# Modulation slots taken in the inverse and ahead of the output matrix, and a first expert that starts without its lead-in

## The chip, the cores and the metric

The kernel runs on one core of one Trainium2 chip. The metric is the device time of one execution in microseconds (us); the figure compared is the median over executions. Five engines share the work: TensorE (PE, with PEld for its weight loads), VectorE (DVE), ScalarE (ACT), GpSimd (POOL) and SyncE (SP), whose queue issues every transfer from memory.

## The reference, cut to what matters

One token sequence (256 tokens, width 1024, fp32) goes through a first block (modulated norm, a gMLP half and an RWKV-7 half, output matrix, router, 32 experts) and then through a two-layer second block (attention and feed-forward). The parts that the change touches:

```
mod = c @ ada_w + ada_b                       # first block's modulation, 1 x 6144
mod2 = silu(c_2) @ w_mod_2[i] + b_mod_2[i]    # second block's, layer i, 1 x 6144
...
state = state * w_t + sa * b_t + v_t * k_t    # RWKV-7, done in chunks of 64 tokens:
                                              # an inverse per chunk and head, then 4 chunks in turn
y = concat(y_a, y_b) @ w_out
x = x + gate1 * y
h = modulate(rmsnorm(x), shift2, scale2)
# router: best group of 4, best 2 experts of its 8, slots sorted by expert
y_e = (silu(xb @ w_gate[e]) * (xb @ w_up[e])) @ w_down[e]      # 32 experts, 6.3 MB of weights each
x = x + gate2 * sum(weights * y_e)
```

## The kernel before, in words

**Weights** stream through a ring of six 2 MB slots (`ring`), filled by SP in one fixed order (`load`, line 302) and used by TensorE in the same order (`take`). Load n waits until `slot_freed` has counted n-5. The first matmul of the next slot's use frees the slot before it (`opened`), so a slot taken earlier lets a later load start earlier. The order of loads is: four of `ada_w`, five of `w_in` and a small one, eight of `ada_w` (numbers 10 to 17), two of `w_mod0`, two of `w_out`, two more of `w_mod0`, then the experts' matrices (`load_matrix`, lines 353 and 366). Each expert has gate, up and down, 2 MB each. The experts use nine places, the six of the ring and three `wide` pairs in the arena, so that the first three experts are loaded before any is freed; the refill of a place waits for the use that follows it.

**Modulation.** A modulation vector is a product with one column, cut in slots: `mod_slice` (line 591) does eight narrow matmuls on one 2 MB slot into bank 0 (`part`), and `fill(n)` does the next n slots wherever it is called. After every fourth slot ScalarE copies the bank (`part_copy`, line 2219), TensorE turns the copy to columns (`flush`, line 604) and VectorE adds the bias (`mod_columns`, line 1506); the first slot of the next four waits for that (`mod_copied`). Slots 4 to 11 are the first block's, 12 to 15 the second block's.

**The inverse** (`inverse`, products at line 783) doubles a block-triangular inverse in six levels l = 0 to 5, for two halves T of 128 tokens. At each level TensorE makes two products that VectorE masks (line 1658, `p_ready`), and after these two or four more that VectorE adds up (lines 1664 and 1667). Engines alternate by semaphores.

**The recurrence** is a chain: `u_of(c)` (line 838), `p_first_half` (827), `v_terms` (811), `d_state` (847), `p_state` (819), `y_state` (863), `y_v` (857), `y_u` (871), each followed by a copy on VectorE (`pb_of`, `u_of`, `state_of`, `y_of`). Fills and flushes stand between them. After it come the group norm's sums (905, 919), the router's small products (911, 914), the output matrix (939 on the gMLP half, 948 on the RWKV half), and the router: logits (975), turned (980), two fills (591), ranks (986 to 990) once VectorE has the one-hots (1781), and one flush.

**The experts.** Tokens are gathered by products into eight chunks (`gather`, 997), ScalarE copies each into `xsT` (2328), and before the first expert `gathered` clears banks 4 to 7 by products with zeros (`add_y` with `first`, 1038). Then `expert(i, e)` reads two numbers from `mtab` (1089, 1090) and runs `window`: gate and up products (1050), the combination of the expert before (`add_y`, 1038), turned activations (1071) and the down product. VectorE copies the window's tokens to `xw` at the start of its `act_pass` (1838). `frees` are the semaphores that tell SP of a free place; that of the up matrix is sent by the first down product. Experts 0 to 4 are written out, the others run in loops of three.

Of the kernel before, what the change touches and what calls it, by code (L numbers as in the profile page):

```python
# [19 lines left out]
ACT = mybir.ActivationFunctionType  # L20
AX = mybir.AxisListType

P = 128
# [3 lines left out]
DC = D // P  # L27
# [5 lines left out]
NE, HID = 32, 512  # L33
# [76 lines left out]
def build_program(nc, a):  # L110
    with ExitStack() as ctx:
# [184 lines left out]
        def _(sp):  # L296
# [36 lines left out]
            for i in range(2):  # L333
                load_mod("w_mod0", i)
            for i in range(2):
                load(w_cols(a["w_out"], 512 * i), 4096)
            for i in range(2, 4):
                load_mod("w_mod0", i)
# [224 lines left out]
        def _(pe):  # L563
# [352 lines left out]
            last.then_inc(S("logits_done"), 1)  # L916
            pe.wait_ge(S("ysq_ready"), 2)
# [35 lines left out]
            ahead[0] = True  # L953
# [28 lines left out]
            fill(2)  # L982
# [3 lines left out]
            mm(bank[6][:, 0:NE], upper[:, :], oh[:, 0], start=True, stop=True).then_inc(S("slot_freed"), 1)  # L986
# [26 lines left out]
            for c in range(4, DC):  # L1013
                pe.wait_ge(S("xs_copied"), c - 3)
                gather(c, 0)
                gather(c, 1).then_inc(S("xs_done"), 1)


            moe_n0 = st_pe.n
            pe.wait_ge(S("mtab_ready"), 1)  # L1020

            def gathered():

                pe.wait_ge(S("routes_copied"), 2)
                pe.wait_ge(S("ym_ready"), 1)
                pe.wait_ge(S("pwin_made"), 1)
                add_y(1, first=True)
                add_y(0, first=True, parts=(1,))
                pe.wait_ge(S("xs_copied"), 8)
                for name in ("up_done", "down_done", "act_turned"):  # L1030
                    pe.nop().then_inc(S(name), 1)
                add_y(0, first=True, parts=(0,))

            def add_y(t, first=False, name=None, parts=(0, 1)):

# [1540 lines left out]
```

## Time and profile before

| | us |
|---|---|
| median of 3 runs | 1507.18 |
| lowest, highest | 1506.53, 1508.94 |
| the profiled execution | 1503.41 |
| span of its instructions | 1501.7 |
| TensorE busy in the span | 1431.7 (95%) |
| VectorE busy | 613.2 (41%) |
| ScalarE busy | 245.1 (16%) |
| GpSimd busy | 210.6 (14%) |

The stages by the clock of the trace: inverse from 143 to 176, recurrence to 206, output matrix 215 to 244, router to 261, gather to 276, experts 280 to 727, second block to the end. TensorE's share says little by itself: in the experts a transfer can set the pace while TensorE is still busy nine tenths of the time. Idle time of TensorE is short everywhere, so the question at each place is what would be late next.

### The profile page before, as it was taken

To read this page: it belongs to the slowest core of one execution; us is meant where nothing else is said; L and a number is where in the kernel's file an instruction comes from. 1 tells how busy PE (TensorE), PEld (TensorE's weight loads), DVE (VectorE), ACT (ScalarE), POOL (GpSimd) and SP (SyncE) were. 2 spreads that over 40 slices of the span, in tenths; PEclk is the share of its full clock that TensorE was granted. 3 is DMA by queue.
4 is the path that set the end of the run, shared out by engine and by line. 5 is a ranking of instruction groups with operands and counts; after the bars stand their busy time and mean duration, and the time that the engine had idled before them with its cause. 6 is when DMAs were issued, how large, how long until landed. Compare 5 with 4: busy or idle time off the path is not lost.

```text
span 1501.7 us, 23350 instructions
## 1 busy us (share of the span) xinstructions
PE 1431.7 (95%) x9316; PEld 940.4 (63%) x9317; DVE 613.2 (41%) x1087; ACT 245.1 (16%) x496; POOL 210.6 (14%) x149
## 2 busy tenths in 40 slices
PE   6999999999999999999899999999999999999997
PEld 3867854544444444444486749998448664899943
DVE  1356544111111111111463425556665463455666
ACT  1230013200000000000301622001031052200001
POOL 2000000000000000000000027770000002577100
PEclk9999999999999999999999999999999999999999
DMA  9664295899999999999999245436426942352610
GB/s 375 242 253 182 74 378 199 329 426 421 425 425 427 423 425 425 424 425 427 409 393 370 79 137 216 153 132 233 164 87 233 402 179 80 105 209 72 236 58 29
DMA packets 91794, 400.91 MB, mean 267 GB/s; under 512 B 7329, under 2 KB 12577, under 8 KB 63553
## 3 DMA queue, kind: packets, MB, share of 16 engines
q1 hardware_dynamic: 91712, 399.73, 67.3%
q8 instruction: 63, 1.03, 0.3%
q14 instruction: 19, 0.15, 0.0%
HBM read 398.66 MB, written 1.05 MB: 266 GB/s over the span
## 4 chain that ended last, share of the span: by engine, by line
PE 78%; DMA 12%; DVE 6%; issue 1%; ACT 1%; SPq 1%; DVEq 0%; ACTq 0%
PE psum L1382 17%; PE psum L1050 16%; PE psum L1434 7%; PE psum L1196 5%; DMA arena<-in_moe_up 4%; PE psum L662 4%; PE psum L1344 4%; PE psum L1038 4%; DMA ring<-in_moe_up 2%; DMA arena<-in_moe_gate 2%; DMA arena<-in_w_mod 2%; PE psum L1414 2%; PE psum L591 2%; PE psum L783 2%; PE psum L1229 2%; PE psum L1214 2%
## 5 line engine op out<-in xcount | busy, mean ns | idle before, releaser
L1050 PE MATMUL psum<-ring,arena 128*64 128x256 f32 (+1 forms) x1760 | 241.4, 427 | 12.5 <-DMA ring<-in_moe_up 6.2
L1050 PEld LDWEIGHTS psum<-ring,arena 128*64 128x64 f32 x1760 | 127.3, 138 | 133.2 <-issue 61.0
L1382 PE MATMUL psum<-arena,ring 128*128 128x128 f32 x1280 | 150.4, 276 | 2.1 <-ACT arena L2198 2.0
L1382 PEld LDWEIGHTS psum<-arena,ring 128*128 128x128 f32 x1280 | 146.5, 192 | 2.8 <-issue 2.8
L1842 DVE TENSOR_TENSOR arena<-psum,arena 128x256 f32<-128x256 f32 x32 | 13.6, 425 | 257.2 <-PE psum L1050 257.2
L1050 PE MATMUL psum<-arena 128*64 128x256 f32 (+1 forms) x800 | 109.1, 425 | 5.1 <-DMA arena<-in_moe_up 3.3
L1382 PE MATMUL psum<-arena 128*128 128x128 f32 x960 | 113.9, 276 | 0.0
L1196 PE MATMUL psum<-arena,ring 128*128 128x256 f32 x512 | 112.7, 382 | 0.8 <-DVE arena L1493 0.7
L557 POOL TENSOR_TENSOR arena<-ring 128x1024 f32<-128x1024 f32 x20 | 47.1, 2353 | 459.1 <-PE psum L1344 242.5
L1382 PEld LDWEIGHTS psum<-arena 128*128 128x128 f32 x960 | 110.4, 192 | 0.0
L1196 PEld LDWEIGHTS psum<-arena,ring 128*128 128x128 f32 x512 | 97.6, 192 | 15.9 <-issue 3.1
L1434 PE MATMUL psum<-arena 128*128 128x512 f32 x220 | 99.3, 594 | 2.1 <-DVE arena L2131 2.1
L1050 PEld LDWEIGHTS psum<-arena 128*64 128x64 f32 x800 | 56.9, 137 | 60.3 <-issue 25.9
L1038 PE MATMUL psum<-arena 64*128 64x512 f32 x272 | 76.9, 640 | 0.7 <-ACT arena L2352 0.7
L1434 PEld LDWEIGHTS psum<-arena 128*128 128x128 f32 x220 | 41.6, 191 | 55.0 <-issue 54.9
L1929 DVE SCALAR_TENSOR_TENSOR arena<-arena,small 128x2048 f32<-128x2048 f32 x27 | 63.5, 2352 | 17.9 <-DMA arena<-in_w_mod 17.2
L2352 ACT ACTIVATE arena<-psum 128x512 f32<-128x512 f32 x32 | 19.1, 597 | 307.6 <-PE psum L1050 307.6
L529 POOL MEMSET arena<- 128x640 f32 x1 | 0.6, 631 | 479.7 <-DVE x L1881 479.7
L662 PE MATMUL psum<-arena,ring 128*128 128x256 f32 x256 | 58.1, 388 | 0.0
L1344 PE MATMUL psum<-ring,arena 128*128 128x512 f32 x128 | 55.5, 594 | 0.6 <-DVE arena L1975 0.6
L662 PEld LDWEIGHTS psum<-arena,ring 128*128 128x128 f32 x256 | 49.8, 195 | 8.4 <-issue 1.6
L1838 DVE COPY arena<-arena 128x512 f32 x32 | 13.7, 427 | 89.7 <-issue 79.1
(423 smaller groups left out, 1728.7 us busy)
## 6 DMA issues: line engine op xcount, KB each, us to landing
ring<-in_moe_gate SPq DMA_DIRECT2D x22, 2048.0 KB, 24.1
ring<-in_moe_up SPq DMA_DIRECT2D x22, 2048.0 KB, 22.7
ring<-in_moe_down SPq DMA_DIRECT2D x22, 2048.0 KB, 24.4
arena<-in_w_mod SPq DMA_DIRECT2D x32, 1024.0 KB, 9.6
ring<-in_ada_w SPq DMA_DIRECT2D x12, 2048.0 KB, 10.7
ring<-in_w_qkv SPq DMA_DIRECT2D x12, 2048.0 KB, 15.0
arena<-in_moe_gate SPq DMA_DIRECT2D x20, 1024.0 KB, 22.2
arena<-in_moe_up SPq DMA_DIRECT2D x20, 1024.0 KB, 20.8
```

Source lines behind the costliest of these rows:

```text
L557: g(nc.gpsimd.tensor_tensor(s1, w21, w22, ALU.add))
L591: last = mm(part[32 * g:32 * g + 1, :], vec[:, c:c + 1], w[:, cc, 512 * g:512 * g + 512], start=(c == 0), stop=(c == DC - 1), tile_positio ...
L662: last = mm(b[:, mi * TOK:(mi + 1) * TOK], w[:, c, m * P:(m + 1) * P], hT[:, c, :], start=(c == 0), stop=(c == DC - 1))
L783: last = mm(out[ps, j * CH:(j + 1) * CH], left(ps, j), right(ps, j), start=True, stop=True, tile_position=(ps.start, ps.start))
L1038: last = mm(bank[4 + 2 * t + n][:, :], pwin[hs, t * P:(t + 1) * P], ym[hs, :], start=first, stop=(name is not None), skip_group_check=True)
L1050: ins = mm(bank[b][o, 0:n], lhsT, w[:, half * n:(half + 1) * n], start=first, stop=last, tile_position=(0, 64 * half))
L1196: last = mm(bank[1 + u % 6][:, mi * TOK:(mi + 1) * TOK], w[:, c, m * P:(m + 1) * P], hTd[:, c, :], start=(c == 0), stop=(c == DC - 1))
L1214: last = mm(bank[1 + u % 6][:, :], hTd[:, c, t * P:(t + 1) * P], w[:, c, :], start=(c == 0), stop=(c == DC - 1))
L1344: last = mm(bank[1 + 2 * t + n][:, :], oT[:, c, t * P:(t + 1) * P], w[n][:, c, :], start=(c == 0), stop=(c == DC - 1))
L1382: last = mm(bank[b + k][:, slot * P:slot * P + P], left[:, k, c], right[:, c, :], start=(c == 0), stop=(c == 3))
L1434: last = mm(bank[t][:, :], *terms[t], start=(p == 0), stop=(p == PAIRS - 1))
L1929: ins = V.scalar_tensor_tensor(out=macc2, in0=w, scalar=by, in1=macc2, op0=ALU.mult, op1=ALU.add)
```

## The change

In the order of the program:

- SP loads all four `w_mod0` slots (numbers 18 to 21) before the two of `w_out` (22 and 23).
- In the inverse, TensorE does a fill between the two masked products of a level and the products behind them, at levels 0, 2, 3, 4 and 5, and the second flush at level 1. VectorE's `mod_columns` goes to level 1.
- The recurrence keeps one fill (slot 12) and one flush of the seven fills and two flushes that stood between line 838's first products and line 911 (slot 13 still stands behind 905). Its products stand in another order, and VectorE's copies with them.
- Slots 14 and 15 are filled before line 919, and the third block of columns is flushed behind 939. In the router four idle products stand in place of the two fills; nothing reads them.
- The gather of chunks 4 to 7 uses the banks in another turn, and the two `mtab` numbers of expert 0 are read before its last chunk. `gathered` is gone: VectorE clears banks 4 to 7 by memsets. The first gate product waits for seven copied chunks, its last eighth for the eighth.
- `act_pass` copies the tokens of the following window after its own multiplication, not its own window's at the start.
- The up matrix's place is told free by the first `add_y` product behind the up products.

```diff
-            for i in range(2):
+            for i in range(4):
                 load_mod("w_mod0", i)
             for i in range(2):
                 load(w_cols(a["w_out"], 512 * i), 4096)
-            for i in range(2, 4):
-                load_mod("w_mod0", i)
...
+                    if l == 1:
+                        flush()
+                    else:
+                        fill(1)
                     for T in range(NT):
                         pe.wait_ge(S("p_ready"), 2 * l + T + 1)
...
             u_of(0)
-            fill(1)
+            flush()
             p_first_half(0)
-            flush()
+            pe.wait_ge(S("xt_ready"), 12)
+            y_v(1)
             u_of(1)
-            pe.wait_ge(S("pb_ready"), 2)
             v_terms(1)
-            fill(1)
             d_state()
-            fill(1)
+            y_u(0)
             p_state()
-            y_u(0)
+            y_state()
             u_of(2)
-            y_v(1)
             fill(1)
             p_first_half(1)
-            y_state()
-            fill(1)
             u_of(3)
             y_u(1)
-            flush()
-            fill(1)
...
             last.then_inc(S("logits_done"), 1)
+            fill(2)
             pe.wait_ge(S("ysq_ready"), 2)
...
+            flush()
             rows(diag[:, 0], 1, 3)
...
-            fill(2)
+            idle_products(3, 4)
...
             rows(diag[:, 1], 2, 3)
-            flush()
...
-                return mm(bank[1 + c % 4][:, :], xr[:, t, :].rearrange("q (p c) -> q c p", c=DC)[:, c, :], perm[:, t, :],
+                return mm(bank[1 + (c + 3 * (c // 4)) % 4][:, :], xr[:, t, :].rearrange("q (p c) -> q c p", c=DC)[:, c, :], perm[:, t, :],
...
             for c in range(4, DC):
-                pe.wait_ge(S("xs_copied"), c - 3)
+                pe.wait_ge(S("xs_copied"), 4)
+                if c == DC - 1:
+                    pe.wait_ge(S("mtab_ready"), 1)
+                    extra0 = pe.value_load(mtab[0:1, NE:NE + 1], min_val=0, max_val=3)
+                    before0 = pe.value_load(mtab[0:1, 2 * NE:2 * NE + 1], min_val=1, max_val=4 * NE)
                 gather(c, 0)
                 gather(c, 1).then_inc(S("xs_done"), 1)
...
+                    if frees and n == 0:
+                        last.then_inc(S(frees), 1)
...
+                        if k == 0 and c == DC - 1:
+                            pe.wait_ge(S("xs_copied"), DC + 1)
                         last = product(1 + k, xw[:, c, :], w(c), 256, c == 0, c == DC - 1)
...
-                add_y(0)
+                add_y(0, frees=frees and frees[2])
...
-                    if frees and k == 0:
-                        last.then_inc(S(frees[2]), 1)
...
-            gathered()
...
+            d(V.memset(bank[6][:, :], 0.0))
+            dve.wait_ge(S("routes_copied"), 2)
+            for b in (5, 7):
+                d(V.memset(bank[b][:, :], 0.0))
+            dve.wait_ge(S("xs_copied"), 5)
+            d(V.memset(bank[4][:, :], 0.0))
             dve.nop().then_inc(S("pwin_made"), 1)
-            dve.wait_ge(S("routes_copied"), 2)
-
-            def act_pass(start, row, done):
-
-                dve.wait_ge(S("up_done"), done)
-                V.tensor_copy(xw, xsT[:, :, bass.ds(start, WIN)]).then_inc(S("xw_ready"), 1)
+
+            dve.wait_ge(S("xs_copied"), DC - 1)
+            V.tensor_copy(xw[:, 0:DC - 1, :], xsT[:, 0:DC - 1, 0:WIN]).then_inc(S("xw_ready"), 1)
+            dve.wait_ge(S("xs_copied"), DC)
+            V.tensor_copy(xw[:, DC - 1, :], xsT[:, DC - 1, 0:WIN]).then_inc(S("xs_copied"), 1)
+
+            def act_pass(following, row, done):
+
...
                 V.tensor_tensor(actm, bank[2][:, 0:4 * WIN], sg, ALU.mult).then_inc(S("act_done"), 1)
+                V.tensor_copy(xw, xsT[:, :, bass.ds(following, WIN)]).then_inc(S("xw_ready"), 1)
...
+            part_copy()
             row_copies(gate1b, 1, 3)
...
-            part_copy()
             row_copies(gate2b, 2, 3)
```

Three places on TensorE show how the rows stand. The first is the inverse up to its end. Line 783 (781 after) is the inverse's product, 591 (589) a fill, 604 (602) a flush, 838 (840) the first product of the recurrence. Before:

```order
L857 MATMUL psum<-arena 64x128 x8
L783 MATMUL psum<-ident,arena 64x64 x64
L783 MATMUL psum<-arena 64x64 x448
L838 MATMUL psum<-arena 64x64 x8
L591 MATMUL psum<-ring,cols 1x512 x8
L827 MATMUL psum<-arena 64x64 x8
```

After:

```order
L859 MATMUL psum<-arena 64x128 x8
L781 MATMUL psum<-ident,arena 64x64 x32
L589 MATMUL psum<-ring,cols 1x512 x8
L781 MATMUL psum<-ident,arena 64x64 x32
L781 MATMUL psum<-arena 64x64 x32
L602 MATMUL psum<-ident,macc 128x4 x4
L781 MATMUL psum<-arena 64x64 x96
L589 MATMUL psum<-ring,cols 1x512 x8
...
L781 MATMUL psum<-arena 64x64 x32
L840 MATMUL psum<-arena 64x64 x8
L602 MATMUL psum<-ident,macc 128x4 x4
```

Five fills and a flush now stand inside the inverse, and a flush stands behind the first product of the recurrence.

The second place is the end of the recurrence, up to the output matrix (939, after 936). 838 and 871 (840 and 873) are `u_of` and `y_u`, 905 and 919 (901 and 916) the group norm's sums. Before:

```order
L838 MATMUL psum<-arena 64x64 x8
L871 MATMUL psum<-arena 64x128 x8
L604 MATMUL psum<-ident,macc 128x4 x4
L591 MATMUL psum<-ring,small 1x512 x8
L905 MATMUL psum<-arena,bones 128x512 x2
L591 MATMUL psum<-ring,small 1x512 x8
L911 MATMUL psum<-modc,arena 128x16 x8
L914 MATMUL psum<-rw,modc 128x36 x8
L919 MATMUL psum<-arena,bones 128x512 x2
```

After:

```order
L589 MATMUL psum<-ring,small 1x512 x8
L829 MATMUL psum<-arena 64x64 x8
L840 MATMUL psum<-arena 64x64 x8
L873 MATMUL psum<-arena 64x128 x8
L901 MATMUL psum<-arena,bones 128x512 x2
L589 MATMUL psum<-ring,small 1x512 x8
L907 MATMUL psum<-modc,arena 128x16 x8
L910 MATMUL psum<-rw,modc 128x36 x8
L589 MATMUL psum<-ring,small 1x512 x16
L916 MATMUL psum<-arena,bones 128x512 x2
```

Nothing stands any more between 829, 840, 873 and 901, which wait for one another's copies on VectorE; two fills stand ahead of 916.

The third place is the last of the gather (997, after 993) and the first gate product (1050, after 1040). Before:

```order
L997 MATMUL psum<-arena 128x512 x8
L1038 MATMUL psum<-arena 128x512 x4
L1089 TENSOR_LOAD level
L1089 ISA x2
L1090 TENSOR_LOAD level
```

After:

```order
L993 MATMUL psum<-arena 128x512 x6
L1013 TENSOR_LOAD level
L1013 ISA x2
L1014 TENSOR_LOAD level
L1014 ISA x2
L993 MATMUL psum<-arena 128x512 x2
L1094 COMPARE_AND_BRANCH
L1095 UNCONDITIONAL_BRANCH
L1047 REGISTER_ALU
L1040 MATMUL psum<-ring,arena 64x256 x32
```

The four zero products are gone and the two loads of a number stand ahead of the last two gather products.

## Rows read from the trace of the kernel before

**Rows 1.** Chain of waits: start, us, what (the last transfer of the experts).

```profile
679.52 37.14 DMA ring<-in_moe_up
716.71 3.67 PE psum L1050 x32
```

**Rows 2.** Windows: stretch, length, busy (x instructions) by engine, clock, DMA share, GB/s.

```profile
290.00:292.00 2.00, 2.00 (x12) 0.63 (x10) 1.03 (x2) 0.00 (x0) 0.00 (x0) 1.00 0.69 295
292.00:294.00 2.00, 2.00 (x10) 0.43 (x6) 0.36 (x1) 0.00 (x0) 0.00 (x0) 1.00 0.68 197
...
566.00:727.00 161.00, 148.51 (x992) 74.44 (x990) 26.13 (x57) 11.22 (x23) 0.00 (x0) 1.00 1.01 424
```

**Rows 3.** Timeline of TensorE, a late expert: start, us, line, operation, count [idle before <-releaser].

```profile
627.81 3.67 PE L1050 MATMUL psum<-ring,arena 128*64 128x256 f32 x32 [1.02 <-DMA ring<-in_moe_up]
```

**Rows 4.** Timeline of SP's queue: the first refills of the ring.

```profile
284.99 0.33 SPq L353 DMA_DIRECT2D ring<-in_moe_gate  x1
291.59 0.33 SPq L353 DMA_DIRECT2D ring<-in_moe_up  x1
294.82 0.38 SPq L353 DMA_DIRECT2D ring<-in_moe_down  x1
```

**Rows 5.** Timeline of TensorE: the inverse, a fill and a flush.

```profile
146.28 1.15 PE L783 MATMUL psum<-ident,arena 64*64 64x64 f32 x32 [0.30 <-DVE arena L1658]
...
155.46 5.82 PE L783 MATMUL psum<-arena 64*64 64x64 f32 x192 [0.43 <-DVE arena L1658]
161.64 5.81 PE L783 MATMUL psum<-arena 64*64 64x64 f32 x192 [0.36 <-DVE arena L1658]
167.82 7.81 PE L783 MATMUL psum<-arena 64*64 64x64 f32 x256 [0.37 <-DVE arena L1658]
...
176.69 1.90 PE L591 MATMUL psum<-ring,cols 128*1 128x512 f32 x16
178.52 1.14 PE L827 MATMUL psum<-arena 64*64 64x64 f32 x16
179.59 1.05 PE L604 MATMUL psum<-ident,macc 128*128 128x4 f32 x8
```

**Rows 6.** Timeline of TensorE: the end of the recurrence.

```profile
201.24 1.09 PE L871 MATMUL psum<-arena 128*64 128x128 f32 x16 [0.86 <-DVE arena L1641]
...
203.74 1.90 PE L591 MATMUL psum<-ring,small 128*1 128x512 f32 x16 [0.43 <-DVE modc L1506]
```

**Rows 7.** Timeline of TensorE: the router, and three idle products of a later place.

```profile
255.73 0.41 PE L986 MATMUL psum<-arena,upper 128*128 128x32 f32 x2 [1.47 <-DVE arena L1781]
...
260.63 7.23 PE L997 MATMUL psum<-arena 128*128 128x512 f32 x16 [1.01 <-DVE arena L1801]
...
734.73 2.84 PE L610 MATMUL psum<-ident 128*128 128x512 f32 x6
```

**Rows 8.** Timeline of TensorE: gather, zero products, experts 0 and 1.

```profile
269.42 7.03 PE L997 MATMUL psum<-arena 128*128 128x512 f32 x16
276.38 2.64 PE L1038 MATMUL psum<-arena 64*128 64x512 f32 x8
280.00 2.77 PE L1050 MATMUL psum<-ring,arena 128*64 128x256 f32 x23 [0.98 <-issue]
283.24 4.75 PE L1050 MATMUL psum<-ring,arena 128*64 128x256 f32 x41 [0.47 <-issue]
...
290.47 10.78 PE L1050 MATMUL psum<-ring,arena 128*64 128x512 f32 x80
```

**Rows 9.** Timeline of ScalarE: the copy of chunk 6.

```profile
274.83 0.78 ACT L2328 ACTIVATE arena<-psum,small 128x512 f32<-128x512 f32 x1 [0.94 <-PE psum L997]
```

**Rows 10.** Timeline of VectorE: the first copy to xw.

```profile
277.67 0.43 DVE L1838 COPY arena<-arena 128x512 f32 x1 [10.55 <-PEq L1031]
```

**Rows 11.** Timeline of TensorE: gate products of a later expert.

```profile
367.52 7.09 PE L1050 MATMUL psum<-ring,arena 128*64 128x256 f32 x48 [2.25 <-issue]
```

**Rows 12.** Windows, columns as in rows 2: the stretch around it.

```profile
360.00:380.00 20.00, 17.75 (x104) 9.82 (x102) 2.67 (x6) 0.98 (x2) 0.00 (x0) 0.91 1.02 424
```

More of the change, by code:

```diff
@@ L952, in _ @@
                     last.then_inc(S("mix_done"), 1)
-            ahead[0] = True
             pe.wait_ge(S("rows_copied"), 2)
@@ L981, in _ @@
             last.then_inc(S("logits_done"), 1)
-            fill(2)
+            idle_products(3, 4)
             pe.wait_ge(S("routed"), 6)
             oh = rt[:, 392:456].rearrange("p (t e) -> p t e", t=NT)
-            mm(bank[6][:, 0:NE], upper[:, :], oh[:, 0], start=True, stop=True).then_inc(S("slot_freed"), 1)
+            mm(bank[6][:, 0:NE], upper[:, :], oh[:, 0], start=True, stop=True)
             mm(bank[6][:, NE:2 * NE], ones[:, :], oh[:, 0], start=True, stop=False)
@@ L1013, in _, with add_y @@
             for c in range(4, DC):
-                pe.wait_ge(S("xs_copied"), c - 3)
+                pe.wait_ge(S("xs_copied"), 4)
[3 more added lines that the diff above has]
+                    before0 = pe.value_load(mtab[0:1, 2 * NE:2 * NE + 1], min_val=1, max_val=4 * NE)
                 gather(c, 0)
                 gather(c, 1).then_inc(S("xs_done"), 1)
+            for name in ("up_done", "down_done", "act_turned"):
+                pe.nop().then_inc(S(name), 1)
             moe_n0 = st_pe.n
[L1020 to L1034, printed above, removed]
-                for n in parts:
+            def add_y(t, name=None, frees=None):
+                for n in range(2):
                     hs = slice(64 * n, 64 * n + 64)
-                    last = mm(bank[4 + 2 * t + n][:, :], pwin[hs, t * P:(t + 1) * P], ym[hs, :], start=first,
+                    last = mm(bank[4 + 2 * t + n][:, :], pwin[hs, t * P:(t + 1) * P], ym[hs, :], start=False,
                               stop=(name is not None), skip_group_check=True)
@@ L1087, in entry @@
                     return mtab[0:1, bass.ds(i * PASS + n, 1)] if e >= FIRST else mtab[0:1, n:n + 1]
-                extra = pe.value_load(entry(NE + e), min_val=0, max_val=3)
-                before = pe.value_load(entry(2 * NE + e), min_val=1, max_val=4 * NE)
+                extra = pe.value_load(entry(NE + e), min_val=0, max_val=3) if e else extra0
+                before = pe.value_load(entry(2 * NE + e), min_val=1, max_val=4 * NE) if e else before0
                 def slots(k, chunks):
@@ L1660, in inverse @@
                             d.to(V.tensor_tensor(Xi[:, T], Pm[:, T], b8(eye), ALU.add), "x_ready")
+                    if l == 1:
+                        mod_columns()
                     for T in range(NT):
@@ L1677, in _ @@
             u_of(1)
+            state_of()
             mod_columns()
-            state_of()
             pb_of(2)
+            y_of(0)
             u_of(2)
-            y_of(0)
             pb_of(3)
@@ L1685, in _ @@
             y_of(1)
-            mod_columns()
             d.to(V.scalar_tensor_tensor(out=modc[:, 0, 32:40], in0=modc[:, 0, 32:40], scalar=1.0, in1=col("norm2_g", 0, 8),
@@ L1856, in _ @@
                 before = dve.value_load(mtab[0:1, bass.ds(i + 2 * NE, 1)], min_val=1, max_val=4 * NE)
+                following = dve.value_load(mtab[0:1, bass.ds(i + 1, 1)], min_val=0, max_val=SLOTS)
                 with dve.If(extra > 0):
                     with dve.Fori(0, extra, 1) as w:
-                        act_pass(nc.s_assert_within(start + w * WIN, 0, SLOTS, skip_runtime_bounds_check_because=within),
+                        act_pass(nc.s_assert_within(start + w * WIN + WIN, 0, SLOTS, skip_runtime_bounds_check_because=within),
                                  nc.s_assert_within(i * 4 + w, 0, 4 * NE - 1, skip_runtime_bounds_check_because=within),
                                  before + w)
-                act_pass(nc.s_assert_within(start + extra * WIN, 0, SLOTS, skip_runtime_bounds_check_because=within),
+                act_pass(following,
                          nc.s_assert_within(i * 4 + extra, 0, 4 * NE - 1, skip_runtime_bounds_check_because=within),
@@ L2327, in xs_copy @@
                 act.wait_ge(S("xs_done"), c + 1)
-                a_.to(A(xsT[:, c, 0:SLOTS], bank[1 + c % 4][:, :], ACT.Identity, bias=modp[:, c, 0:1],
+                a_.to(A(xsT[:, c, 0:SLOTS], bank[1 + (c + 3 * (c // 4)) % 4][:, :], ACT.Identity, bias=modp[:, c, 0:1],
                         scale=modp[:, c, 1:2]), "xs_copied")
```

## The prediction, made before the changed kernel was run

> **What bounds the kernel now.** I read from the end of the experts backwards, because the change stands ahead of them and everything behind them is untouched. The chain of waits [rows 1] shows a transfer in the middle of it: the last up matrix lands at 716.7, and TensorE starts on it at once. The windows [rows 2] show why: from 566 to 727 the transfer engines are full (share 1.01, 424 GB/s) while TensorE has 12.5 us of idle time in 161. The timeline agrees, a late expert's up products wait 1.02 us for their matrix [rows 3]. So the end of the experts is set by a stream of transfers. Nine places are loaded before expert 0 frees any; 86 more matrices of 2.097 MB land by 716.7, at 424 GB/s 4.95 us each, 425 us. The first of them is issued at 284.99 [rows 4], 431.7 us ahead of that landing. The stream therefore runs nearly without a break from the first refill on, and **the time of the kernel moves with the moment of the first refills**, not with TensorE's speed inside the experts. The first refill is told by the first up product of expert 0. So I follow TensorE from the inverse to that product, and ask at each edit whether TensorE was the late one there.
>
> In the inverse it mostly was: its waits on VectorE's masks are 0.30, 0.43, 0.36 and 0.37 us, and levels 1 and 5 show none [rows 5]. In the recurrence fills and flushes hide VectorE's copies almost everywhere, with 0.86 and 0.43 us left [rows 6]. In the router VectorE is late: TensorE idles 1.47 us before the ranks and 1.01 us before the gather [rows 7].
>
> **The inverse.** A fill costs 178.52 - 176.69 = 1.83 us from start to start, a flush 1.05 with 0.07 of overlap, 0.98 [rows 5]. Five fills and one flush enter: 9.15 + 0.98 = 10.13. They cover the four waits, 1.46 together, since each stands in front of the products that wait. VectorE's part of a level is shorter than TensorE's lengthened one, so nothing else becomes late. The moved column step on VectorE is one small operation and waits for a flush that runs beside its own masks. Net **+8.67**. If the fills hid nothing it would be +10.1.
>
> **The recurrence, up to the output matrix.** Seven fills and two flushes stood here (12.81 + 1.96 = 14.77); four fills (slots 12 to 15) and one flush stand here now (7.32 + 0.98 = 8.30). That is -6.47. Their cover goes with them. The two old waits (0.86 and 0.43) fall away, and three new ones appear at the end, where the next product needs the copy of the one just before: u_of(3) behind p_first_half(1), y_u(1) behind it, and the mean sums behind that. One such turn shows as 0.86 idle [rows 6], so 2.58 against 1.29, +1.29. The others are covered: the flush behind u_of(0), y_v(1) and v_terms(1) behind the next ones, y_u(0) beside the state's copy, and fill 12 behind u_of(2). Net **-5.18**, between -6.5 (no new wait) and -4.3 (a fourth turn).
>
> **Behind it.** The third flush now stands between the two halves of the output matrix, where TensorE is never idle: **+0.98**. ScalarE's part copy moves ahead of its gate rows and has the 14 us of line 939 for itself. The output matrix is now loaded last: its second slot is issued when fill 12 begins, some 20 us before it is wanted (that fill, the products behind it and fills 13 to 15), against 5 us for 2 MB at the stream's rate. It stays hidden. If it did not, the wait would stand before line 939, and it would be the first thing to look for.
>
> **The router.** Two fills (3.66) make way for four idle products, 0.95 each by three that took 2.84, 3.8 in all. Behind either TensorE waits for VectorE, 1.47 us now [rows 7], so 1.3 then: **0**. The flush that goes stood before a wait of 1.01 us for the same VectorE chain: it only lengthens that wait, **0**. This is the point of the account: 4.6 us of work leave a place where they cost nothing and go to places where they cost all but a part. The gather so ends later by 8.67 - 5.18 + 0.98 = **+4.5 us**.
>
> **The first expert.** The gather ends at 269.42 + 7.03 = 276.45 and the first gate product starts at 280.00 [rows 8]. Between them are the zero products and 0.98 us of loading two numbers. Afterwards nothing stands there. The tokens are ready: chunk 6 is copied at 275.61 [rows 9], seven eighths of VectorE's copy take 0.38 [rows 10], so xw is there at about 276.1. Chunk 7 follows 1.8 later and is wanted 3.1 us into the gate products. The memsets lie on VectorE, idle 10.55 us there [rows 10]. The two loads of numbers move ahead of the last chunk; the 80 products without a gap from expert 0's down into expert 1's [rows 8] have two such loads inside and show no stall when work is queued. So **-3.55**; if the 0.98 stays, -2.57. The stall of 0.47 inside the gate products [rows 8] I keep; at best it goes too.
>
> **The second refill** is issued at 291.59, 1.1 us behind the first down product [rows 4, 8]. It will be told by a product that starts at 287.99, and so be issued about 2.5 us sooner relative to the first. The transfer engines have shares of 0.69 and 0.68 between 290 and 294 [rows 2], 1.26 us of rest that this fills. The third refill, at 294.82, comes just in time behind two in a row. **-1.3**, between 0 and -1.6. Later frees come sooner too, but there the stream is full. The earlier copy to xw inside each expert hides nothing that is late now: 0.
>
> **Sum.** 4.5 - 3.55 - 1.3 = -0.35. The profiled execution took 1503.41, with a span of 1501.7 and 1.7 around it: it would take 1503.0. It lies 3.8 under the median of 1507.18; taking the shift over, 1506.8.
>
> **A row that speaks against it.** A wait of 2.25 us in an expert is followed by 48 products in 7.09 us [rows 11], where 32 take 3.67 [rows 3], so 48 about 5.5; the granted clock of that stretch is 0.91 [rows 12], part of it at 1.2 GHz instead of 2.4. The price was 1.6 us. The three new waits make 2.6 us of idle, but in three pieces with products between. The router's pieces of 1.47 and 1.01 brought no fall. I take no fall.
> By the Trainium skill (TensorE: Matmul & The Clock Gate, "HAM oscillation — how this bites in real kernels") waits between short bursts of products can drop the clock each time. By that page the end of the recurrence would be slow and the result would be that of rival B; this case's trace has one such fall, after a single long wait.
>
> **The rivals.**
> A. The new turns of the recurrence do not appear, because VectorE's copies finish under the products, and the stall of 0.47 goes: -0.35 - 2.58 - 0.47 = -3.4, 1503.8, faster. For it: fills hide such copies wholly now. Against: the last three products each read the copy of the one before. 0.14.
> B. The clock falls at the end of the recurrence, +1.6: about +1.3, 1508.5. Still no measurable change. 0.13.
> C. The first expert does not start sooner in effect: the gate products wait for the copies or the numbers, or the stream starts at a time that something else sets, above all the last half matrix that SP issues at the gather's end, ahead of every refill. Then the cost of the fills stands alone, up to +4.5, 1511.7, slower. It decides from where less than 1.5 of the 4.85 us is kept. Against: the half matrix needs 2.5 us at 424 GB/s and the first refill comes some 4 us behind it. 0.14.
> D. The experts are TensorE's to bound after all, and an earlier end of the stream is not used: the rows of 566 to 727 exclude it, 0.01.
> Forecast: 0.58.
>
> **How the numbers follow.** A measurement of this kernel tells about 0.2%, 3.0 us, from no change. The forecast and B lie inside it; some of A and C does too, and their ends are outside. That gives 0.16 faster, 0.69 same, 0.15 slower. The range reaches from A's end, 1503.5, to near C's, 1511.0.
>
> **What would show it.** In the changed trace: inverse about 8.7 us longer and without waits on the masks; three waits of 0.86 before the mean sums; line 939's successor starting 3.5 us later; the wait before the ranks still above 1; gate products directly behind the gather; two refills about 4 us apart instead of 6.6; transfers without rest from then on, and the last up matrix landing within 1 us of 716.7. Wrong would be: a wait for the output matrix, a clock under 1.00 between 195 and 280, or a stall of the gate products behind the gather.

## The result and the profile after

The changed kernel took **1516.76 us** (median of 17; 1509.41 to 1521.80), the kernel before, run beside it, 1507.52 (median of 17): a ratio of 1.0045, 95% interval 1.0028 to 1.0061. It is slower, by some 7 to 9 us, and outside the predicted range. The profiled execution took 1520.43, with a span of 1518.7. It is among the longest of its kernel, as that of before (1503.41) was among the shortest, so the 17 us between the two traces show where the time goes better than how much it is.

Spans and mean granted clocks of the two, before and then after:

```profile
core 0: 1501.7 us, clock 0.993
```
```profile
core 0: 1518.7 us, clock 0.985
```

The inverse of the changed kernel in TensorE's timeline (start, us, ... [idle before <-releaser]); 589 is a fill:

```profile
142.55 2.08 PE L781 MATMUL psum<-ident,arena 64*64 64x64 f32 x64
144.56 1.90 PE L589 MATMUL psum<-ring,cols 128*1 128x512 f32 x16
...
165.46 1.20 PE L781 MATMUL psum<-arena 64*64 64x64 f32 x34 [1.52 <-issue]
...
174.17 2.80 PE L589 MATMUL psum<-ring,cols 128*1 128x512 f32 x16
...
182.52 2.20 PE L781 MATMUL psum<-arena 64*64 64x64 f32 x68 [1.78 <-issue]
...
188.57 1.11 PE L840 MATMUL psum<-arena 64*64 64x64 f32 x16
```

The mask waits of [rows 5] are gone, as forecast. In their place stand two stalls for which the profile shows no releaser ("issue"), and one fill of 2.80 where the others take 1.90. The inverse ran from 142.81 to 175.65 before, 32.84 us, and takes 46.02 now.

The end of the recurrence, the router and the first gate products:

```profile
195.47 3.67 PE L813 MATMUL psum<-arena 128*128 128x64 f32 x16
...
210.24 1.14 PE L840 MATMUL psum<-arena 64*64 64x64 f32 x16 [0.86 <-DVE arena L1625]
212.23 1.97 PE L873 MATMUL psum<-arena 128*64 128x128 f32 x16 [0.86 <-DVE arena L1630]
215.07 3.78 PE L901 MATMUL psum<-arena,bones 128*128 128x512 f32 x4 [0.86 <-DVE arena L1638]
...
229.76 13.90 PE L936 MATMUL psum<-ring,arena 128*128 128x512 f32 x32
...
271.68 0.41 PE L983 MATMUL psum<-arena,upper 128*128 128x32 f32 x2 [1.38 <-DVE arena L1771]
...
276.48 9.09 PE L993 MATMUL psum<-arena 128*128 128x512 f32 x16 [0.69 <-DVE arena L1791]
...
287.12 7.03 PE L993 MATMUL psum<-arena 128*128 128x512 f32 x16
294.08 6.26 PE L1040 MATMUL psum<-ring,arena 128*64 128x256 f32 x56
```

Three turns of 0.86; no wait for the output matrix (936); the gate products directly behind the gather, without the 0.98 and the 0.47 of [rows 8]. But the sums of 901 take 3.78 where the same form takes 1.96 at 916, `v_terms` (813) takes 3.67 where it took 2.00, and the first half of the gather 9.09 against 7.23 [rows 7]. The windows (columns as in rows 2) say why: in these stretches the mean granted clock is near half, so most of them ran at 1.2 GHz instead of 2.4.

```profile
191.00:202.00 11.00, 11.00 (x76) 10.48 (x75) 1.39 (x2) 0.00 (x0) 1.87 (x5) 0.53 0.15 56
212.00:219.00 7.00, 5.90 (x24) 2.86 (x28) 2.46 (x6) 0.00 (x0) 0.00 (x0) 0.51 0.38 141
273.00:281.00 8.00, 7.31 (x10) 2.84 (x10) 6.97 (x18) 1.19 (x2) 1.52 (x3) 0.57 0.44 186
```

The first refills (SP's queue) and the last up matrix (chain of waits) of the changed kernel, and the stream between them in the windows of after and then of before:

```profile
298.23 0.33 SPq L351 DMA_DIRECT2D ring<-in_moe_gate  x1
302.29 0.33 SPq L351 DMA_DIRECT2D ring<-in_moe_up  x1
...
730.11 3.67 PE psum L1040 x32
...
298.23:730.11 431.88, 410.67 (x2787) 208.56 (x2783) 70.29 (x155) 30.39 (x62) 0.00 (x0) 1.00 1.01 422
```
```profile
284.99:716.71 431.72, 415.54 (x2786) 206.28 (x2782) 73.20 (x155) 30.39 (x62) 0.00 (x0) 1.00 1.00 421
```

The refill is 13.24 later, the last up matrix 13.40: the time of the kernel does move with the first refill. The stretches of the two profiled executions, each cut where the first product of the next one starts, or at the issue of the refill:

| stretch | before | after | difference | forecast |
|---|---|---|---|---|
| start to the inverse | 142.81 | 142.55 | -0.3 | 0 |
| inverse | 32.84 | 46.02 | **+13.2** | +8.7 |
| to the end of the gather | 100.73 | 105.51 | **+4.8** | -4.2 |
| to the first refill | 8.61 | 4.15 | -4.5 | -3.6 |
| to the last up matrix | 431.72 | 431.88 | +0.2 | -1.3 |
| to the end | 784.99 | 788.59 | +3.6 | 0 |

The change does not touch the last stretch. Apart from its last few us, its clock stood at 1.2 GHz for 13.7 us in the trace of after and for 6.8 in that of before, which at half speed makes 3.4 of the 3.6.

### The profile page after: what moved, and what is told of

Same layout as the page of the kernel before. It is cut to its first block, busy times and chain, and to the rows that moved or that the text cites. A ratio compares the mean times of both kernels' runs of the same rounds, so it can differ in the third digit from the quotient of the medians.

```text
span 1518.7 us, 23453 instructions
## 1 busy us (share of the span) xinstructions
PE 1442.2 (95%) x9316; PEld 948.4 (62%) x9317; DVE 613.2 (40%) x1093; ACT 245.1 (16%) x496; POOL 210.5 (14%) x149
## 3 DMA queue, kind: packets, MB, share of 16 engines
q8 instruction: 63, 1.03, 0.3%
## 4 chain that ended last, share of the span: by engine, by line
PE 74%; DMA 16%; DVE 6%; issue 1%; ACT 1%; SPq 1%; DVEq 0%; ACTq 0%
PE psum L1371 17%; PE psum L1040 13%; DMA ring<-in_moe_up 12%; PE psum L1423 7%; PE psum L1185 5%; PE psum L660 4%; PE psum L1333 4%; PE psum L1026 3%; PE psum L781 2%; DMA arena<-in_w_mod 2%; PE psum L589 2%; PE psum L1403 2%; PE psum L1218 2%; PE psum L1203 2%; DMA ring<-in_ada_w 1%
## 5 line engine op out<-in xcount | busy, mean ns | idle before, releaser
L1040 PE MATMUL psum<-ring,arena 128*64 128x256 f32 (+1 forms) x1760 | 238.2, 424 | 14.1 <-DMA ring<-in_moe_up 9.0
L2492 ACT ACTIVATE arena<-arena 128x256 f32<-128x256 f32 x44 | 18.3, 417 | 189.7 <-DVE arena L2086 189.7
```

The costliest lines, as they stand in the source:

```text
L1040: ins = mm(bank[b][o, 0:n], lhsT, w[:, half * n:(half + 1) * n], start=first, stop=last, tile_position=(0, 64 * half))
```

## The experiments

Parts of the change: D is the first expert's start, I the inverse and the recurrence, S the two slots ahead of the output matrix with the idle products. "Before" is always the kernel before, run on the same chip beside them. A bare turn is a product that waits for VectorE's copy of the product just before it, with nothing between. Each expectation gives its theories letters of its own and says what they mean. My own text uses two: A, transfers that start inside the inverse stall TensorE, and B, the bare turns lower the clock.

**D alone, I alone, S alone.**

> The kernel before with the gather and first-expert part of the change alone (memsets for the zero products, numbers of expert 0 read before the last chunk, tokens of the next window copied ahead, up matrix freed at the first combination product). Theory A (the sum was right there, the loss is in the front): the first refill of the ring is issued about 4 us sooner than in the kernel before, 281 instead of 285, and the kernel is 3.5 to 5 us faster, about 1503. Theory B (the first expert's part is where the loss is): no gain or slower, 1507 or more.

> The kernel before with the inverse and recurrence part alone: five fills and a flush inside the inverse, the recurrence in its new order, slots 14 and 15 still in the router. By the sum of the prediction this is -0.2 us (8.67 - 10.13 + 1.29), no change. Theory A (stalls of TensorE without a releaser while the transfer engines are full during the inverse, and clock falls behind the stalls and the three bare turns): stalls of 3 to 3.5 us in the inverse appear again, some stretches at 1.2 GHz between 190 and 220, and the kernel is 3 to 10 us slower, about 1513. Theory B: 1507.

> The kernel before with the third part alone: all four slots of the second block loaded and filled ahead of the output matrix, third flush between its halves, four idle products in the router. The sum says +4.6 us (two fills 3.66 and a flush 0.98 that had stood beside VectorE's router steps), about 1512, the same under both theories; if theory A's clock falls also come here (no bare turn, no busy transfers in the inverse) it would be more than that.

D: 1502.60 against 1506.50, ratio 0.9976 [0.9954, 0.9999]. I: 1515.32, 1.0059 [1.0035, 1.0083]. S: 1519.29, 1.0084 [1.0061, 1.0107], which is more than the +4.6 of its fills and flush (from 6 executions only). D's lines show the gate products right behind the gather; I's show the stalls, at the places where the changed kernel has them:

```profile
280.21 7.03 PE L997 MATMUL psum<-arena 128*128 128x512 f32 x16
287.17 7.13 PE L1044 MATMUL psum<-ring,arena 128*64 128x256 f32 x64
```
```profile
165.38 1.21 PE L783 MATMUL psum<-arena 64*64 64x64 f32 x34 [1.68 <-issue]
182.44 2.20 PE L783 MATMUL psum<-arena 64*64 64x64 f32 x68 [1.78 <-issue]
```

So the stalls come with the fills of the inverse, and S has a loss of its own.

**The transfers taken out of the inverse.** A fill that stands earlier frees its slot earlier, so SP, which had issued nothing between the eighth `ada_w` load and line 591's fills, now loads `w_mod0` during the inverse: the transfer engines' share from 142 to 190 is 0.63 where it was 0.30. The changed kernel with SP held until the inverse has ended:

```diff
             for i in range(4, 12):
                 load_mod("ada_w", i)
+            sp.wait_ge(S("xt_ready"), 12)
             for i in range(4):
                 load_mod("w_mod0", i)
```

> The changed kernel, with one wait more on SP: the loads of the second block's slots start only when the inverse has ended. Theory A: the transfer engines are idle during the inverse, its two stalls of 1.52 and 1.78 us go, with them the clock fall behind 190 in most executions; 3 to 7 us faster than the changed kernel, 1510 to 1514. Theory B (the stalls belong to the code of the inverse with fills in it, whatever the transfers do): they stay, time as the changed kernel, about 1517.

1508.66, ratio 1.0004 [0.9985, 1.0023]: one line of SP gives back most of the loss. All inverse products run without a stall, and every fill takes 1.90; the inverse is 41.09 long, 8.25 more than before:

```profile
162.43 5.82 PE L782 MATMUL psum<-arena 64*64 64x64 f32 x192
170.00 5.81 PE L782 MATMUL psum<-arena 64*64 64x64 f32 x192
177.57 5.82 PE L782 MATMUL psum<-arena 64*64 64x64 f32 x192
```

**The transfers put in without the fills.** The kernel before, with four extra 2 MB loads during the inverse (8 MB that nothing reads; the work of TensorE and VectorE is unchanged):

```diff
+            sp.wait_ge(S("pv_done"), 1)
+            for k in range(4):
+                sp.dma_start(ring[:, 0, :] ..., a["w_mod1"] ...).then_inc(S("out_stored"), 16)
+                sp.wait_ge(S("out_stored"), 16 * (k + 1))
```

> The kernel before with four extra loads of 2 MB (read and never used) into a slot that is empty during the inverse; nothing on TensorE or VectorE differs, no fill stands in the inverse. Theory A (a full set of transfer engines holds up what TensorE needs to go on in the inverse): one to three stalls without a releaser among the inverse's products, each 1 to 2 us and ending where a load ends, 2 to 5 us slower than the kernel before. Theory B (the stalls came with the fills' code): no stall, no change.

1516.75 against 1508.75, ratio 1.0054 [1.0032, 1.0076]. The waits of TensorE (total, times, longest) and windows of 1 us around the first stall:

```profile
PE psum L789 <- issue: 6.0, 4, 1.6
```
```profile
154.47 5.60 PE L789 MATMUL psum<-arena 64*64 64x64 f32 x184 [1.49 <-issue]
```
```profile
151.00:152.00 1.00, 1.00 (x42) 1.00 (x40) 0.90 (x2) 0.00 (x0) 0.00 (x0) 1.00 1.03 434
152.00:153.00 1.00, 0.98 (x30) 0.83 (x26) 0.76 (x2) 0.00 (x0) 0.00 (x0) 1.00 1.06 426
153.00:154.00 1.00, 0.00 (x0) 0.00 (x0) 0.41 (x1) 0.00 (x0) 0.00 (x0) 1.00 0.99 418
154.00:155.00 1.00, 0.53 (x19) 0.53 (x20) 0.00 (x0) 0.00 (x0) 0.00 (x0) 1.00 0.28 115
```

Four loads, four stalls, one more than I expected. **Theory A is shown**: transfers beside the inverse's small products cost, with or without fills. The inverse is 39.41 long here, 6.57 more than before. The time rises by 8.0, of which the table below puts 6.2 to the work at equal clock.

My expectation that each stall ends with its load came true only for the first. The second goes on when its load is over, and the third begins after its load, while the transfer engines rest (their share is the last number but one):

```profile
163.00:164.00 1.00, 0.00 (x0) 0.00 (x0) 0.36 (x1) 0.00 (x0) 0.00 (x0) 1.00 0.08 16
172.00:174.00 2.00, 0.71 (x24) 0.57 (x18) 1.62 (x4) 0.00 (x0) 0.00 (x0) 1.00 0.00 0
174.04 4.12 PE L789 MATMUL psum<-arena 64*64 64x64 f32 x127 [1.33 <-issue]
```

So TensorE is not slowed by the traffic as such; a load holds up something that TensorE runs out of a little later (see the last section).

**What lowers the clock besides.** Two tries on the held changed kernel: idle products that read real tokens instead of the identity, and fills 13 to 15 moved into the three bare turns.

> The kernel of e4 with the router's four idle products on the normed tokens instead of the identity (which is zero in 127 of 128 places); same shapes, same count. Theory C (products on zeros do not hold the clock as the fills did): no clock fall behind the router's wait, where e3, e4 and the changed kernel each show one; mean clock up by 0.002, 2 to 3 us faster than e4, about 1506. Theory D (the fall there comes from the waits, or by chance): as e4, 1508.7.

> The kernel of e4 with fills 13, 14 and 15 moved into the three bare turns at the end of the recurrence. The turns' 2.6 us of waits go. If those waits were also what made the clock fall behind 205, 1.7 us more at the mean sums: 2.6 to 6 us faster than e4, 1503 to 1506. If fills do not hide a turn, as e4.

1506.06, ratio 0.9992 [0.9970, 1.0014], and 1507.59, 0.9988 [0.9970, 1.0007]. Neither differs from the held kernel by more than the intervals. In the profile of e6 the clock still fell behind the router's wait (261 to 264 us). In e7 the fills did hide the turns, but fills 14 and 15 came before their slots did: with SP held, these transfers start some 40 us later.

```profile
206.61 1.90 PE L590 MATMUL psum<-ring,small 128*1 128x512 f32 x16 [0.43 <-DMA ring<-in_w_mod]
211.63 2.44 PE L590 MATMUL psum<-ring,small 128*1 128x512 f32 x16 [2.09 <-DMA ring<-in_w_mod]
```

The two waits, 2.52 together, eat the 2.58 of the three turns. e10 below has them too (0.91 and 2.09).

**A better mixture.** D and I, SP held, `y_state` and fill 13 in two of the turns, and slots 14 and 15 in the router as before, so without S:

> A version meant to beat both: first expert's part (e1), fills in the inverse and the new recurrence (e2) with loads held as in e4, slots 14 and 15 left in the router where they cost nothing, y_state and fill 13 in two of the three bare turns. At equal clock: -4.3 (e1) - 0.2 - 1.7 = about -6, near 1501, below e1's 1502.6. If the clock stays as low as in e4 it is 1504 to 1505, no better than e1.

**1498.06** against 1508.75, ratio 0.9928 [0.9901, 0.9955]: faster than both kernels. At equal clock it is 6.7 below the kernel before, where I had forecast about 6; the rest is a clock higher than that of before. It still has two waits of the length of a turn, but 10 us apart and not three in a row. Its recurrence and router, the clock of 190 to 285, and its refill:

```profile
core 0: 1498.2 us, clock 0.994
```
```profile
200.67 1.14 PE L843 MATMUL psum<-arena 64*64 64x64 f32 x16 [0.84 <-DVE arena L1628]
201.74 1.90 PE L592 MATMUL psum<-ring,small 128*1 128x512 f32 x16
...
210.58 1.98 PE L905 MATMUL psum<-arena,bones 128*128 128x512 f32 x4 [0.86 <-DVE arena L1641]
...
253.63 3.61 PE L592 MATMUL psum<-ring,small 128*1 128x512 f32 x32
258.72 0.41 PE L985 MATMUL psum<-arena,upper 128*128 128x32 f32 x2 [1.47 <-DVE arena L1774]
...
190.00:285.00 95.00, 90.01 (x515) 55.89 (x517) 42.36 (x103) 22.87 (x40) 5.05 (x12) 1.00 0.84 335
...
283.51 0.33 SPq L354 DMA_DIRECT2D ring<-in_moe_gate  x1
```

The router's two fills again end in front of the 1.47 of VectorE, at no cost.

**This kernel taken apart.** Three runs change one thing in it (e9, e12, e13), two change the router's products in e7 (e10, e14), and one puts the hold alone into the kernel before (e11).

> The kernel of the run before it in this study (e8: inverse with fills, two covered turns, the two slots in the router, direct expert, SP held until the inverse has ended) without the one line that holds SP. Theory A (transfers that start inside the inverse stall TensorE there, and the stalls bring a fall of the clock behind them): three stalls of together 3.3 us return in the inverse, the time rises by 3.3 at equal clock and by some 1 to 3 more by a lower mean clock, so 1502 to 1505 where e8 took 1498.1, ratio to before 0.996 to 0.998. Rival (the falls behind the stalls were chance, the stalls alone cost): 3.3, ratio 0.995, mean clock as e8's 0.9936. Rival (the hold only pushes the work of the transfers to a later place where it costs the same): no change, ratio 0.993.

> The kernel e7_cover (changed kernel, SP held, fills 13 to 15 in the three bare turns) without the four idle products in the router; what TensorE does there is then only to wait some 5 us. If the idle products keep the clock up, the mean clock falls below e7's 0.9906 and the time rises by 1.3 us for each 0.001, the first ranks and the gather in front of it at 1.2 GHz: 1510 to 1512, ratio 1.001 to 1.003. If they do nothing for it, or hurt it (theory C of the earlier runs: products of zeros and ones do not count as work), the time stays at e7's ratio, 0.9988, or goes under it. The work they stand in front of cannot start sooner in either case, since VectorE is late there.

> The kernel before with the one line that holds SP until the inverse has ended, and nothing else. In the kernel before no slot is freed inside the inverse, so SP has nothing to issue there: the line should do nothing, ratio 1.000. Rival: the hold gains by itself, by an amount that would then have to be taken off what e4 and e8 showed for it (0.997 or less).

> e8 (inverse with fills and SP held, direct expert, slots 14 and 15 in the router) with the three turns at the end of the recurrence bare, as the changed kernel has them: y_state ahead of u_of(2), fill 13 behind the mean sums. At equal clock one more wait of 0.86 us than e8, so +0.9. Theory B (the short waits in a row lower the clock): mean clock under e8's 0.9936, about 0.991, and 1.4 us for each 0.001, ratio 0.996 to 0.997. Theory S (it is the two slots taken away from the router that lower it, not the turns): mean clock as e8's, ratio 0.9935.

> e8 with only slot 14 used ahead of the output matrix (loaded ahead of it too), slot 15 still in the router. At equal clock +1.8 us, the fill that leaves a place where it costs nothing. Theory S (fewer products in the router, longer rest there, lower the clock): half of the step from e8 (0.9936) to e7 and e10 (0.9906, 0.9912), so 0.992, +2 more, ratio 0.9955. Theory that S's loads or its flush behind the first half of the output matrix lower the clock, not the fills' place: mean clock as e8's, ratio 0.994.

> e7 (changed kernel, SP held, turns covered) with 32 one-column products on the real tokens in the router in place of the four idle ones: the form and number of the products of two fills, with no slot behind them; nothing reads them. Theory S in its narrow form (it is the fills that keep the clock in the router, idle products of zeros and ones do not): mean clock rises from 0.9906 to e8's 0.9936, ratio 0.9955. If instead the clock stays at 0.991 as with idle products (e7) and with none (e10), what TensorE does in the router has nothing to do with it, ratio 0.9985, and the lower clock comes from the two fills, or their loads, ahead of the output matrix.

Within the executions of one kernel the time follows the mean granted clock: 1.35 us for each 0.001 (277 executions of these kernels, each taken against its own kernel's mean; standard error 0.03). The table gives the mean clock (standard error 0.0003 for before, 0.0004 to 0.0010 for the others) and the mean time moved by that slope to a clock of 0.990 (standard error 0.1 for before, 0.2 to 0.5 for the others). That slope is an average over all places of the kernel; a fall where TensorE is not the late one may cost less.

| kernel | ratio to before, 95% | mean clock | time at 0.990 |
|---|---|---|---|
| before (111 executions) | 1 | 0.9915 | 1510.5 |
| changed | 1.0045 [1.0028, 1.0061] | 0.9881 | 1512.6 |
| D alone (e1) | 0.9976 [0.9954, 0.9999] | 0.9914 | 1505.4 |
| I alone (e2) | 1.0059 [1.0035, 1.0083] | 0.9894 | 1514.3 |
| S alone (e3) | 1.0084 [1.0061, 1.0107] | 0.9862 | 1513.1 |
| before, with four loads more (e5) | 1.0054 [1.0032, 1.0076] | 0.9894 | 1516.7 |
| changed, held (e4) | 1.0004 [0.9985, 1.0023] | 0.9892 | 1506.6 |
| held, idle products on tokens (e6) | 0.9992 [0.9970, 1.0014] | 0.9902 | 1507.4 |
| held, turns covered (e7) | 0.9988 [0.9970, 1.0007] | 0.9906 | 1508.3 |
| as e7, no idle products (e10) | 0.9986 [0.9966, 1.0006] | 0.9912 | 1507.6 |
| as e7, 32 narrow products in their place (e14) | 0.9987 [0.9966, 1.0008] | 0.9927 | 1510.7 |
| mixture (e8) | 0.9928 [0.9901, 0.9955] | 0.9936 | 1503.8 |
| mixture, not held (e9) | 0.9990 [0.9969, 1.0011] | 0.9921 | 1508.9 |
| mixture, three bare turns (e12) | 0.9943 [0.9927, 0.9959] | 0.9923 | 1504.4 |
| mixture, slot 14 ahead of the output matrix (e13) | 0.9947 [0.9925, 0.9969] | 0.9924 | 1504.3 |
| before, held (e11) | 1.0004 [0.9977, 1.0030] | 0.9907 | 1510.8 |

- The hold alone does nothing (e11). Without it the mixture takes 7.2 us more by means (e9), against the 4.3 to 6.3 that I expected: its inverse is 45.83 long against 41.09, which is 4.7 of it, and its clock, lower by 0.0015 (standard error 0.0009), makes 2.0 more.
- Three bare turns in a row (e12): 0.0013 less clock than the mixture, with a standard error of 0.0006, and 2.3 us more by means. That is half of what I had put down for theory B, and by itself no more than a hint.
- Slot 14 away from the router (e13): 0.0012 less clock, with the same error. Its 1.8 us are not seen: 0.5 at equal clock.
- e7 and e10 lie 0.0030 and 0.0024 under the mixture, but not for the slots alone, since they have the waits for late transfers besides. Between them, with and without idle products, there is no difference clear of the error (0.0006, standard error 0.0008). Real tokens in the wide products (e6, 0.9902 against 0.9892) are within the error as well.
- The narrow products on tokens hold the clock, 0.0021 over e7 with a standard error of 0.0008. They take 7.05 us where two fills take 3.61, end 2 us late for the ranks, and so bring nothing. Whether it is their data, their form, their length or the missing wait that holds the clock stays open.

**Where the falls lie.** Every profile shows the stretches at 1.2 GHz. They come by chance in part, but at three places they go with the edits:

| place | kernels | profiles with a fall there |
|---|---|---|
| behind the inverse (it starts at 180 to 194 us) | stalls in it (changed, e2, e5, e9) | 4 of 4, 6.8 to 10.2 us long |
| | fills in it, SP held (e4, e6, e7, e8, e10, e12, e13, e14) | 1 of 8 (e14) |
| | as before, no loads in it (before, e1, e3, e11) | 3 of 4 |
| in the end of the recurrence | three bare turns (changed, e2, e4, e6, e12) | 5 of 5, 3.4 to 6.8 us |
| | e8's order (e8, e9, e13) | 0 of 3 (e13 has one a little later) |
| | turns covered by fills (e7, e10, e14) | 2 of 3, behind the waits for transfers |
| | order of before (before, e1, e3, e5, e11) | 2 of 5 |
| at the router's wait and the gather | both slots filled there (before, e1, e2, e5, e8, e9, e11, e12) | 1 of 8 (e12) |
| | one slot (e13) or nothing (e10) | 2 of 2 |
| | four wide products (changed, e3, e4, e6, e7) | 4 of 5 |
| | 32 narrow products (e14) | 0 of 1 |

The turns of e12 and the same stretch of e8, which differ in the place of two calls:

```profile
201.00:207.00 6.00, 5.01 (x20) 2.74 (x20) 1.72 (x5) 0.00 (x0) 0.00 (x0) 0.50 1.06 401
```
```profile
200.00:212.00 12.00, 10.47 (x108) 6.16 (x109) 4.38 (x8) 0.00 (x0) 0.00 (x0) 1.00 1.04 392
```

This and the means together speak for theory B and for the fills in the router. The first place is less clear: a fall follows the stalls, but the inverse of before, which has neither fills nor stalls, has one behind it in three profiles of four.

By single differences from the mixture (-0.0015, -0.0013, -0.0030) the changed kernel should have 0.9878, and it has 0.9881. That is closer than the numbers allow: the sum has an error of 0.0014, its last term is made with the late transfers, which the changed kernel does not have, and the parts taken from the other side do not add up (D, I and S alone lose 0.0075 of clock together, the whole change 0.0034). At equal clock they do: -5.1, +3.8 and +2.6 make +1.3, and the changed kernel has +2.1.

## Why the prediction was wrong

By means (1515.3 against 1508.5) the changed kernel is 6.8 slower. Of that the clock, 0.0034 lower, makes 4.6 by the slope, and 2.1 remain at equal clock, where I had -0.35. By the items below it should be +4.6 (-0.35, the stalls +4.93, the fills -0.42, the first expert -0.9, the second refill +1.3). The 2.5 between them are not explained; 2.0 of it may go with S, which alone is at +2.6 where its fills and flush were priced at +4.6.

- **The inverse**: the fills' +8.67 was right as far as it went; 8.25 was measured where nothing disturbs it (e4). The step that failed is "nothing else becomes late". I moved each fill as work of TensorE and left out what the fill releases: its slot, SP's next load, and 2 MB of transfers beside dense small products. That is 4.93 (46.02 - 41.09, the second from the held kernel). It is the largest miss, and the rival list had nothing like it.
- **The recurrence**: the three waits came as forecast, 0.86 each. What failed is "I take no fall". The row that I named against it [rows 11, 12] was the right one. Rival B had the mechanism, priced at one fall of 1.6 us; all five profiles with bare turns have it, at 3.4 to 6.8 us, and the trace of the changed kernel has two falls more, behind the inverse and at the gather. How much of the 0.0034 each place makes is not settled. The range of this item had a slip too: with no new wait it is -6.47 - 1.29 = -7.8 and not -6.5. The result does not hang on it.
- **Behind it**: the output matrix is not waited for, the flush costs its 0.98. Right.
- **The router**: 0 was right for the time of its fills: the wait before the ranks is 1.38. What they did for the clock there I did not see, since no row of before shows the router without them. This step rests on the profiles and on e13 and e14, not on e7 and e10.
- **The first expert**: -3.55 forecast, -4.5 in the trace, of which 0.47 is the stall that went too. D alone confirms it, with -5.1 at equal clock.
- **The second refill**: the refills are 4.06 apart, as forecast, but the -1.3 did not come: 431.88 from the first refill to the last up matrix against 431.72. The transfer engines still rest behind the first refill (share 0.80 from 298 to 302), and what the earlier second refill brought was lost again at a place that no row here names.
- **The frame** held: the end moves with the first refill. And my base was a quick execution: its clock of 0.993 stood over its kernel's mean of 0.9915, so it showed fewer falls than a usual one. Reading "no fall between 195 and 280" as this kernel's habit was a second part of the same error; the unchanged stretch shows falls there in other executions (e1: 209 to 216 us; e11: 218 to 222).

## What to carry to other kernels

When work that frees a buffer is moved, write down the transfer that it starts and what that transfer then runs beside; a wait on the issuing queue is a cheap way to keep the work's new place and the transfer's old one. Then look where the held transfer is wanted: in e7 and e10 it came 0.4 to 2.1 us late. Filler work in a place where an engine waits anyway is free and may hold the clock up; moved out, it may cost both its length and that. Where a gain of a few us rests on the clock, take its mean from many executions, not from the one that is profiled.

## What the hardware showed

- TensorE stalled 1.3 to 1.8 us at a time, with nothing in the program to wait for, when 2 MB loads filled the transfer engines during its densest stretch of small products (e5: 42 products and 40 weight loads in 1 us). Beside the recurrence, at some 10 products in 1 us, full transfer engines brought no such stall (e4, 190 to 206 us, share 1.00).
- The queues in the changed kernel from 174 to 183 us show the instruction stream as transfers of its own:

```profile
q1 hardware_dynamic: 304, 2.24, 65.1%
q8 instruction: 1, 0.02, 0.7%
```

  In the inverse of the held kernel (e4) a packet of queue 8 starts every 3.8 to 5.6 us. With loads beside it the longest steps are 5.7 to 7.2 us: four in the changed kernel, three in e5. Six of these seven end in a stall or in the long fill: the packets that start at 163.1, 173.7 and 180.3 us in the changed kernel, and at 162.1, 171.6 and 177.3 in e5. (The seventh, up to 152.4, costs 0.24 us; the first stall of e5 stands behind a packet at 152.0 after a step of 4.0.) In all six stalls TensorE goes on 1.2 to 1.5 us after such a packet has landed, in e5's third with no load under way. So the stall fits TensorE running out of instructions whose transfer came late. It is still my reading: the profile names no engine for these packets, and no run changed the instruction stream alone. By the Trainium skill instruction memory is refilled in 16 KiB blocks (Runtime: NRT & Kernel Launch, "Terms"), and a transfer engine takes turns between its queues a whole packet at a time (DMA: Bandwidth & Descriptors, "Queues, rings and completion order"). The traces agree with the size, 63 packets of queue 8 with 1.03 MB in the changed kernel; how the queues take turns no run shows.
- A fall of the clock to 1.2 GHz that lasts 3.4 us is 0.0011 of the mean clock of this kernel, 1.5 us by the slope. Those of the changed kernel at 192, 212 and 274 us lasted 10.2, 6.8 and 6.8.
- Four idle products on the identity, 3.70 us of TensorE at full width, did not hold the clock (e7 0.9906, e10 without them 0.9912).
